# Windowed attention woven into its projection panels, a query norm summed as columns, and folds one panel forward

## The reference

```python
xs = xs + g1 * token_mixer(hx, lw, rope, k_c, v_c)
hx = modulate(rmsnorm(xs, norm2_g[l]), sh2, sc2)      # the query norm: its result goes into peer_wq
...
q, k, v = split_qkv(h, w_in)                          # 16 query heads, 4 key heads, 64 wide
s = einsum(q, k) * 64 ** -0.5 - slope * dist          # blocks of 128 queries see 256 keys, the first 128
m = max(max(s), sink); p = exp(s - m)
denom = sum(p) + exp(sink - m)
o = einsum(p / denom, v); y = o @ w_out
```

## Time and profile before

| | us |
|---|---|
| median of 3 runs | 2536.35 (2536.2 to 2538.89) |
| the profiled execution | 2536.2 |
| its span | 2534.4 |
| PE busy | 2441.7 (96%) |
| DVE busy | 1682.5 (66%) |
| ACT busy | 928.1 (37%) |
| chain that ended last | PE 87%, DVE 9%, ACT 2%, issue 1% |

### The profile page before, as it was taken

The page is one execution under the profiler, slowest core; times in us unless marked ns, Lnnn a source line. Parts: engine busy times, 40 slices in busy tenths (PEclk is TensorE's granted clock), DMA queues, the critical chain, the costliest instruction groups (busy, mean ns, idle before and its releaser), DMA issues.

```text
span 2534.4 us, 35089 instructions
## 1 busy us (share of the span) xinstructions
PE 2441.7 (96%) x12016; PEld 2072.3 (82%) x12016; DVE 1682.5 (66%) x3142; ACT 928.1 (37%) x1319; POOL 740.1 (29%) x646
## 2 busy tenths in 40 slices
PE   6999999898999999999999999999999979999998
PEld 4877878686887888888888899999999756788886
DVE  4887769688566667677642478888887685444434
ACT  4223853523233333333333333333333464222222
POOL 0000000000006666676676257777641000000000
PEclk8999999999999999999999999999999999999999
DMA  6222913254234444444456689999997202222321
GB/s 257 100 73 93 350 34 129 95 190 159 100 111 139 139 148 141 150 138 149 139 171 193 206 295 366 365 366 362 360 363 258 76 25 67 91 99 91 100 99 58
DMA packets 177221, 433.59 MB, mean 171 GB/s; under 512 B 32752, under 2 KB 81904, under 8 KB 176752
## 3 DMA queue, kind: packets, MB, share of 16 engines
q1 hardware_dynamic: 123888, 331.61, 37.8%
q0 software_dynamic: 34816, 67.41, 7.7%
q10 hardware_dynamic: 18432, 33.56, 3.6%
HBM read 371.48 MB, written 61.01 MB: 171 GB/s over the span
## 4 chain that ended last, share of the span: by engine, by line
PE 87%; DVE 9%; ACT 2%; issue 1%; DMA 1%; SPq 0%; ACTq 0%; DVEq 0%
PE ps L466 17%; PE ps L467 17%; PE ps L468 17%; PE ps L802 9%; PE ps L803 9%; PE ps L801 9%; PE ps L712 2%; DVE wlo L1398 1%; DVE ar L1451 1%; PE ps L696 1%; PE ps L704 1%; PE ps L781 1%; DVE ar L1513 1%; ACT whi L936 1%; DVE rstd L1412 1%
## 5 line engine op out<-in xcount | busy, mean ns | idle before, releaser
L1398 DVE TENSOR_TENSOR wlo<-raw,whi 128x1024 fp32r<-128x1024 f32 x426 | 521.4, 1224 | 569.7 <-ACT whi L936 568.2
L2239 POOL DMA_INDIRECT w_scratch<-ar x384 | 418.8, 1091 | 953.5 <-DVE wlo L1398 854.3
L936 ACT ACTIVATE whi<-raw 128x1024 fp32r<-128x1024 f32 x424 | 448.9, 1059 | 660.0 <-PE ps L803 403.4
L466 PE MATMUL ps<-b_hi,whi 128*128 128x512 f32 x1328 | 519.6, 391 | 3.2 <-DVE wlo L1398 3.0
L468 PE MATMUL ps<-b_hi,wlo 128*128 128x512 f32 x1328 | 517.6, 390 | 0.0
L467 PE MATMUL ps<-b_lo,whi 128*128 128x512 f32 x1328 | 517.3, 390 | 0.0
L801 PE MATMUL ps<-a_hi,whi 128*128 128x384 f32 x1024 | 342.7, 335 | 0.0
L803 PE MATMUL ps<-a_hi,wlo 128*128 128x384 f32 x1024 | 342.1, 334 | 0.0
L802 PE MATMUL ps<-a_lo,whi 128*128 128x384 f32 x1024 | 342.1, 334 | 0.0
L466 PE MATMUL ps<-a_hi,whi 128*128 128x512 f32 x816 | 326.9, 401 | 8.9 <-DVE wlo L1398 7.2
L467 PE MATMUL ps<-a_lo,whi 128*128 128x512 f32 x816 | 319.6, 392 | 0.0
(11 more groups left out here) (265 smaller groups left out, 2988.7 us busy)
## 6 DMA issues: line engine op xcount, KB each, us to landing
raw<-panels SPq DMA_DIRECT2D x430, 512.0 KB, 3.4
gelu_scratch<-ar ACTq DMA_DIRECT2D x128, 256.0 KB, 2.1
w_scratch<-rstd SPq DMA_DIRECT2D x32, 768.0 KB, 10.9
ar<-w_scratch SPq DMA_DIRECT2D x128, 192.0 KB, 4.7
ar<-gelu_scratch SPq DMA_DIRECT2D x128, 192.0 KB, 5.6
ar<-mod SPq DMA_DIRECT2D x32, 512.0 KB, 5.6
ar<-panels SPq DMA_DIRECT2D x3, 2048.0 KB, 16.0
w_scratch<-ar POOLq DMA_INDIRECT x384
```

The costliest lines, as they stand in the source:

```text
L466: pe.matmul(bank, w_h, hi[:, k, :], start=(k == 0), stop=False)
L936: act.activation(whi[:, u % SPLIT, :], raw[:, u % RAW, :], ACT.Copy).then_inc(hi_ready, 1)
L1398: dve.tensor_tensor(wlo[:, u % SPLIT, :], raw[:, u % RAW, :], f32(whi[:, u % SPLIT, :]), ALU.subtract).then_inc(lo_ready, 1)
L2239: nc.gpsimd.indirect_dma_start(experts, bass.IndirectOffsetOnAxis(offs[:, k:k + 1], 0), vals[:, k:k + 1], None)\
```

## The change

Three things are edited. The sums of the query norm become four columns of 1 (one for each 128 tokens) instead of a 128 x 512 tile, root and reciprocal work on 128 x 4, and four matmuls with the identity spread the factor over the partitions. One fold of the WO loop goes to the CO loop, the others one panel forward, with PE's sums and SP's loads (`pair_at`) to match. The attention's order is written out by hand on three engines: the panels come as p0 = keys of kt 0, p1 = values 0, p2 to p5 = queries of kt 0, p6 = keys of kt 1, p7 = values 1, p8 to p11 = queries of kt 1; the groups run kt 0 first, from block 3 to block 0; pieces of attention stand between the panels from p6 on, and four half panels of SO in its tail. The sink is now taken in by one operation on DVE instead of two. `swa_panel_hi(p)` is ACT's copy of panel p, `swa_panel_lo(p)` DVE's low half; p12 is the first SO panel.

```diff
--- before.py
+++ after.py
-SWB = (0, 2, 3, 1)
+SWB = (0, 2, 3, 1, 0, 2, 3, 3, 3, 3, 3, 3)
+SW_ORDER = (0, 2, 4, 5, 6, 7, 1, 3, 8, 9, 10, 11)
...
-        v2_feat_sb = area(A_S2, 2, T)
+        v2_feat_sb = nt[:, :, :]
...
+        def values_bank(m):
+
+            return 2 if m < 3 else 2 + m % 2
...
-            pair_at = {3: 2, 4: 3, 8: 4, 9: 5, 11: 6, 12: 7, 13: 8, 14: 9, 19: 10, 20: 11, 21: 12, 22: 13, 23: 14, 24: 15}
+            pair_at = {3: 2, 4: 3, 8: 4, 9: 5, 11: 6, 12: 7, 13: 8, 14: 9, 16: 10, 18: 11, 19: 12, 20: 13, 21: 14, 22: 15}
...
+            for n, w in enumerate(SW_ORDER):
+                sp.wait_ge(lo_ready, SW + n - RAW + 1 - U)
+                sp.dma_start(raw[:, (SW + n) % RAW, :], panels[SW + w]).then_inc(landed[(SW + n) % RAW], 16)
...
-                if k in (3, 5):
-                    mod2_sums((k + 5) // 2)
-            norm_total(2, rstd[:, :])
+                if k in (1, 4, 6):
+                    mod2_sums({1: 4, 4: 5, 6: 6}[k])
+            pe.wait_ge(sq_used, 3 * KT - 1)
+            for t in range(TT):
+                pe.matmul(ps[:, 4, t:t + 1], rstd[:, t * P:(t + 1) * P], ones[:, 0:1], start=(t == 0), stop=False)
+            pe.wait_ge(sq_ready, 3 * KT)
+            for t in range(TT):
+                last = pe.matmul(ps[:, 4, t:t + 1], sq[:, (KT - 1) % 2, t * P:(t + 1) * P], ones[:, 0:1], start=False, stop=(t == TT - 1))
+            last.then_inc(sq_used, 1)
+            pe.wait_ge(rstd_ready, 3)
+            for t in range(TT):
+                last = pe.matmul(ps[:, 5, t * P:(t + 1) * P], root_col[:, t:t + 1].to_broadcast([P, P]), ident, start=True, stop=True)
+            last.then_inc(root_out, 1)
             pe.wait_ge(mod_done, 4)
-            mod2_sums(6)
...
+            def swa_panel(p):
+                first = p == 0
+                panel(SW + p, p % 4, ps[:, SWB[p], :], a_hi, a_lo, r_of(SW) + (p + 1 if p < 7 else p + 4), (h_ready, 3 * KT) if first else None,
                       (lambda k: norm_stat(3, k, bank=1)) if first else None)
...
+            def turn_v(u, bank):
                 pe.wait_ge(v2_feat, u + 1)
                 for s in range(TT):
-                    last = pe.transpose(ps[:, 4 + u, s * P:(s + 1) * P], v2_feat_sb[:, u, s * P:(s + 1) * P], ident)
+                    last = pe.transpose(ps[:, bank, s * P:(s + 1) * P], v2_feat_sb[:, u, s * P:(s + 1) * P], ident)
                 last.then_inc(v2_turned, 1)
-            groups = [(b, kt, half) for b in range(TT) for kt in range(2) for half in range(2)]
+
...
+                if m == 0:
+                    pe.wait_ge(v2_done, 2)
+                elif m < 3:
+                    pe.wait_ge(o2, m)
+                else:
                     pe.wait_ge(o2, m - 1)
+                if m == 3:
+                    pe.wait_ge(bank_free, r_of(SW) + 16)
...
+            def out_half(u, half):
+                if half == 0:
+                    pe.wait_ge(lo_ready, SO + u + (1 - U))
+                    pe.wait_ge(bank_free, r_of(SO) + u + 1)
+                    pe.wait_ge(bias2, 4 * len(groups))
+                    pe.wait_ge(o2, TT)
+                else:
+                    pe.wait_ge(o2, 2 * TT)
+                for k in range(4 * half, 4 * half + 4):
+                    last = split3(ps[:, 4 + u, :], u, k, b_hi[:, k, :], b_lo[:, k, :], k == 0, k == KT - 1)
+                if half:
+                    last.then_inc(used, 1)
+            swa_panel(0)
+            swa_panel(1)
+            swa_panel(2)
+            turn_v(0, 4)
+            pe.wait_ge(rt_ready, 4)
+            swa_panel(3)
+            swa_panel(4)
+            norm_total(4, rstd1, bank=6)
+            swa_panel(5)
+            swa_panel(6)
+            pe.wait_ge(v2_done, 1)
+            pe.wait_ge(rt_ready, 5)
+            pe.wait_ge(bank_free, r_of(SW) + 10)
+            swa_scores(0)
+            swa_panel(7)
             swa_scores(1)
+            swa_panel(8)
+            swa_turn(0)
+            turn_v(1, 2)
+            swa_scores(2)
+            swa_turn(1)
+            swa_panel(9)
+            swa_values(0)
+            swa_turn(2)
+            swa_scores(3)
+            swa_turn(3)
+            swa_panel(10)
+            swa_turn(4)
+            swa_values(1)
+            swa_turn(5)
+            swa_panel(11)
+            swa_turn(6)
+            pe.wait_ge(bank_free, r_of(SW) + 16)
+            swa_scores(4)
+            swa_values(2)
+            swa_turn(7)
+            swa_scores(5)
+            swa_values(3)
+            swa_turn(8)
+            swa_scores(6)
+            swa_turn(9)
+            swa_scores(7)
+            swa_turn(10)
+            swa_values(4)
+            swa_turn(11)
+            swa_turn(12)
+            swa_values(5)
+            out_half(0, 0)
+            swa_turn(13)
+            swa_turn(14)
+            swa_values(6)
+            out_half(1, 0)
+            swa_turn(15)
+            swa_values(7)
+            out_half(0, 1)
+            out_half(1, 1)
+            for k in range(2, KT):
+                panel(SO + k, k % 4, ps[:, 4 + k % 4, :], b_hi, b_lo, r_of(SO) + k + 1)
...
-            norm_root(2, rstd[:, :])
+            act.wait_ge(sq_used, 3 * KT)
+            act.activation(root_col, ps[:, 4, 0:TT], ACT.Sqrt, bias=EPS, scale=1.0 / D).then_inc(rt_ready, 1)
...
+            for n in range(4):
+                bias_tiles(n)
+                swa_panel_hi(6 + n)
+            bias_tiles(4)
             swa_exp(0)
             swa_exp(1)
+            swa_panel_hi(10)
+            swa_exp(2)
+            swa_exp(3)
+            swa_out(0)
+            swa_panel_hi(11)
+            swa_out(1)
+            swa_exp(4)
+            swa_exp(5)
+            swa_hi(0)
+            swa_out(2)
+            swa_panel_hi(12)
+            swa_out(3)
+            swa_exp(6)
+            swa_exp(7)
+            bias_tiles(5)
+            swa_out(4)
+            swa_hi(1)
+            swa_out(5)
+            bias_tiles(6)
+            bias_tiles(7)
+            swa_out(6)
+            swa_hi(2)
+            swa_out(7)
+            swa_exp(8)
+            swa_hi(3)
+            swa_exp(9)
+            swa_out(8)
+            swa_exp(10)
+            swa_out(9)
+            swa_exp(11)
+            swa_out(10)
+            swa_exp(12)
+            swa_hi(4)
+            hi_next(0, SO, 0)
+            swa_out(11)
+            swa_exp(13)
+            swa_exp(14)
+            swa_out(12)
+            swa_hi(5)
+            swa_exp(15)
+            swa_out(13)
+            swa_out(14)
+            swa_hi(6)
+            swa_out(15)
+            swa_hi(7)
...
-                if k < 4:
+                if k < 5:
                     fold_half(2 + k // 2, k % 2)
...
-                if k < 6:
-                    fold_half(4 + k // 2, k % 2)
+                if k < 5:
+                    fold_half(4 + (k + 1) // 2, (k + 1) % 2)
...
-            norm_rstd(2)
-            norm_apply(2, x, lambda k: gs2[:, k:k + 1], lambda k: mod[:, 3 * KT + k, 0:1], b_hi, b_lo, middle=lambda: lo(WQ + 1, 1))
+            norm_rstd(2, root_col)
+            dve.wait_ge(root_out, 1)
+            norm_apply(2, x, lambda k: gs2[:, k:k + 1], lambda k: mod[:, 3 * KT + k, 0:1], b_hi, b_lo, r=ps[:, 5, :], middle=lambda: lo(WQ + 1, 1))
...
-                dve.tensor_tensor(tiny[:, o:o + 4], tiny[:, o:o + 4], col("sinks", h, 4), ALU.max).then_inc(mx2, 1)
-                dve.wait_ge(mx2, n + 1)
-                dve.tensor_scalar(tiny[:, o + 4:o + 8], tiny[:, o:o + 4], -1.0, None, ALU.mult).then_inc(nmx2, 1)
-                dve.tensor_tensor(tiny[:, o + 12:o + 16], col("sinks", h, 4), tiny[:, o:o + 4], ALU.subtract).then_inc(nmx2, 1)
+                dve.scalar_tensor_tensor(tiny[:, o + 4:o + 8], tiny[:, o:o + 4], -1.0, less_sinks[:, h:h + 4], ALU.mult, ALU.min).then_inc(nmx2, 1)
+                dve.wait_ge(nmx2, 2 * n + 1)
+                dve.tensor_tensor(tiny[:, o + 12:o + 16], col("sinks", h, 4), tiny[:, o + 4:o + 8], ALU.add).then_inc(nmx2, 1)
...
+            swa_panel_lo(1)
             norm_rstd(3)
+            swa_panel_lo(2)
+            key2(0, 0)
+            swa_panel_lo(3)
+            value2(0, 1)
+            swa_panel_lo(4)
             for k in range(1, KT - 1):
                 add_sq(4, k, rstd1)
+            query2(0, 2)
+            value2_out(0, 4)
+            swa_panel_lo(5)
+            query2(1, 3)
...
+            query2(2, 4)
+            dve.tensor_scalar(less_sinks[:, :], col("sinks", 0, NH2), -1.0, None, ALU.mult).then_inc(mx2, 1)
+            swa_panel_lo(6)
+            norm_rstd(4, rstd1)
+            query2(3, 5)
+            swa_panel_lo(7)
+            residual(0, 4)
+            key2(1, 6)
+            swa_panel_lo(8)
+            dve.wait_ge(mx2, 1)
+            dve.wait_ge(bias_ready, NH2 // 2)
+            pair_bias(0)
+            value2(1, 7)
+            swa_panel_lo(9)
+            pair_bias(1)
+            pair_norm(0)
+            query2(4, 8)
+            swa_panel_lo(10)
```

(76 more changed lines are left out.)

80 lines of the change are left out of this document (19 added, 61 removed).

## The result

The changed kernel takes 2548.9 us (median of 5 runs, 2547.4 to 2552.52) against 2536.35 for the kernel before (5 runs, 2536.1 to 2540.2): ratio 1.0044, 95% interval 1.0032 to 1.0057. It is slower by 0.44%, more than the 0.2% that tells from no change, and lies above the range's end of 2546. The profiled execution took 2547.4, its span is 2545.6.

A forecast was written before the change was run, and what follows sets the result against it. PE, on nearly the whole chain, was taken as the bound, with only its idle stretches to win. 2536.2 - 3.6 (norm and folds) + 1.9 (region without clock) + 3.6 (clock) = 2538.1 us, no change; range 2524 to 2546.

The forecast's parts named there:

- the play of the queues: Attention among the panels: engine orders played with traced prices; 10.4 us of PE waits for ACT, 17.9 in the tail.
- Those of 1.5 to 2.6 I leave at full speed: Attention: PE waits of 1.5 to 2.6 us were taken to cost no clock afterwards.
- two falls in the tail: Attention's tail: waits of 4.2 and 5.2 us drop the clock, adding 0.5, 1.5, 0.5 and 1.2, given as 3.6 us.
- Panels at half clock: Panels among the attention: seeing them run at half clock was named as showing the forecast wrong.
- the second rival: Waits between panels: the clock falls there too, 2.2 us each; 2544.8 with three falls; slower, with some of another rival, 0.29.
- the 2.99 that cost nothing: Elsewhere in the trace: after 2.99 us idle PE came back at full speed, held against clock falls between panels.
- its figure for five falls: Waits between the panels: if the clock falls in all five, the kernel takes 2549 us.
- The region without the clock: Panels and attention, clock effects left out: 1.9 us longer than before.
- The two terms: Panels and attention: 1.9 us longer without the clock, plus 3.6 us for slow clock.
- Norm and folds: Folds and query norm: norm 4.3 us shorter, folds 0.5 late; WQ panels start 3.6 us earlier.
- the third rival: Query norm gives nothing, its end only moving the wait to PE's late WO 7: 2541.7; mostly within no change, 0.37.
- The faster rival: Attention: ACT is not late and panels fill the waits: 2527.7, or 2524 with full clock in the tail; chance 0.34.

The follow-up runs named there:

- keep_warm: The changed kernel with 18 useless matmuls put into six of PE's waits, no other instruction changed; 1.0019 of the kernel before, 2542.0 us.
- after_again: The changed kernel, unaltered, measured again beside variants on their chip; 1.0036 of the kernel before, 2548.4 us.
- no_fold: The changed kernel without the folds' move and with ACT's outs ahead of exponentials and copies; 0.9977 of the kernel before, 2530.8 us.
- sums_later: act_order with PE's sums of the moved fold behind WO panel 3 again, folds left forward; 0.9964 of the kernel before, 2526.75 us.
- act_order: The changed kernel with each `swa_out` ahead of exponentials and copies it doesn't need, `swa_hi` and SO 1's copy placed likewise; 0.996 of the kernel before.

## Why the prediction was wrong

The forecast was 1.9 us over the profile before, and 11.2 were measured. Of the miss of 9.3, 6.4 lie in the region, 4.4 in norm and folds, and -1.5 ahead of any edited work.

- **Waits: right.** Those of ACT and DVE are where the play of the queues put them: turn 1 2.93 (forecast 2.4), values 0 2.12 (2.1), turn 4 2.21 (2.2), scores 7 2.06 (2.6), turn 8 4.32 (4.2), turn 12 4.03 (5.2). In sum 23.7 us of the attention are idle in the changed kernel, not 28: turn 3's wait of 1.5 is gone and turn 5's is 0.39, because slow panels before them took that time.
- **The clock: the step that failed.** "Those of 1.5 to 2.6 I leave at full speed", and 3.6 us for two falls in the tail (its four terms add up to 3.7). Between p8 and p11 the clock fell three times, behind the waits of 2.93, 2.12 and 2.21 (0.72, 0.68 and 0.58 in the rows above), where the forecast had none; in the tail, scores 7 and turn 10 were slow too. Panels at half clock were the prediction's own sign of being wrong. Keeping PE busy in the waits takes 7.4 us out of the region, and removing the waits themselves takes 7 to 10 of busy time beside 9 of idle.
- **The row it leaned on was misread.** Against the second rival, which had 0.29 with "slower", stood one row: "the 2.99 that cost nothing". Its matmul does come at full clock, but the row shows that one alone. What follows it in the same trace of before is slow, from 1.2 us behind the wait for 3 us:

```profile
44.99 0.41 PE L537 MATMUL ps<-a_lo,whi 128*128 128x512 f32 x1
45.21 0.61 PE L538 MATMUL ps<-a_hi,wlo 128*128 128x512 f32 x1
...
48.19 0.60 PE L536 MATMUL ps<-a_hi,whi 128*128 128x512 f32 x1
48.61 0.41 PE L537 MATMUL ps<-a_lo,whi 128*128 128x512 f32 x1
```

```profile
44.00:48.00 4.00, 4.00 (x12) 0.65 0.00 0
```

By the clock of 0.65 over 4 us the wait cost about 1.4 us, an estimate from that row. So it had not cost nothing, and the one argument against the second rival was none. The second rival's mechanism is what happened. That its figure for five falls, 2549, is also the measured time is luck: three falls came between the panels, and 4.4 us of the miss are the norm's and the folds'. The Trainium skill (TensorE: Matmul & The Clock Gate, Part 1), which the prediction weighed, warns that idle gaps between bursts cost clock; keep_warm agrees, at 0.99 for 0.92. That the switch isn't tied to the kernel's own start, which the Trainium skill adds there, no run here shows.
- **The region without the clock: 1.9 forecast, 4.4 measured** (keep_warm's 210.0 less 205.6, with what its matmuls overrun and one fall left behind turn 5, 0.72 over 6 us). The two terms give 5.5 in the forecast, 11.9 in the profile.
- **Norm and folds: -3.6 forecast, +0.8 measured** (+1.8 in after_again)**.** The reciprocal is 0.18 as said. From x's last tile to the spread's end are 4.2 us, not 3.2 (the small sums 1.05 each time, not 0.5). The larger part is the sums ahead of WO 2: their wait of 1.99 was forecast as 1.8, its price not: behind it the clock fell here too, and WO 2 took 7.1 us and not 5.4. x's last tile came 161.6 us after the convolution's sums, not 158.6 (the forecast's 609.4 less 450.8). So the third rival's result, that the norm gives nothing, came true, with PE late from WO 2 on. With the sums where they had been, the stretch is 3.6 us shorter than before the change (179.9 against 183.5), the size of my term by another way.
- **Unforecast, and cancelling:** -1.6 between the key stage and SW, +1.6 at the end. Both are one thing. PE waits 2.1 us for a low half at about 815 us and 2.2 in GU, before and after the change. Behind the first the clock is 0.57 for 4 us in the kernel before and in no_fold, and 1.00 in the changed one and in sums_later; behind the second it is 1.00 in the kernel before and 0.57 in the changed one.

The faster rival (ACT not late, 2524 to 2528) was wrong for this change, and right about what lay in its reach: its condition, ACT's outs in time, is what act_order makes true, and sums_later, which also puts the sums back, then measures 2526.75.

## What to carry to other kernels

Price a wait of PE at up to twice its length: what stands behind it may run at half speed, and here removing 9.2 to 9.4 us of waits took 7.1 to 10.0 us of busy time with it. And when a row is to show that a wait cost nothing, read the granted clock of the next microseconds too, not the first instruction alone. When small pieces go between panels, write the helper's queue (here ACT) so that what PE needs next stands ahead of anything that waits for PE itself or can be done later. And where a wait can't be removed, matmuls into a free bank in it can be worth more than the time they take.

## What the hardware showed that I had not expected

Whether a wait of 2.0 to 2.2 us costs clock isn't told by its length or by the work next to it. The rows, each the first 4 us of panel work behind such a wait in GU, are 0.57 in the changed kernel (2175.6) and in keep_warm (2171.1):

```profile
2171.10:2175.10 4.00, 3.96 (x10) 0.57 0.55 153
```

and 1.00 in the kernel before, in no_fold (2160.0) and in sums_later:

```profile
2156.20:2160.20 4.00, 3.95 (x17) 1.00 0.47 148
```

A fall there leaves 10 or 11 matmuls in 4 us instead of 17 or 18, and costs 1.6 us of the stretch, 370.0 against 368.4. It came out the same in both profiles of the changed kernel.

The fall can also come late. The 4.33 us ahead of turn 8 were followed by a turn of 1.20 in act_order and of 1.97 in sums_later, with the same attention code; but scores 6 behind it were 3.53 and 3.79, so the clock fell in both. Their regions are 198.3 and 200.9: 1.1 of the difference lies between turn 8 and the wait of 1.42 us for DVE's `b_lo` (line 2228), and 1.5 behind that wait, where the next 4 us run at 1.00 in act_order and at 0.60 in sums_later.

What decides it beside the length stays open: no run here varied the moment of a wait alone. A profile is one execution, and executions of one kernel differ in this too: of 22 of the kernel before on one chip, those with a mean granted clock of 0.988 took 2533.1 to 2536.8 us, those with 0.986 took 2536.7 to 2540.0. A difference of 1.6 us between two profiles is therefore no statement about the edit.
